# Nine of twelve wide weight slabs multiplied unsplit in fp32, eight slots for the modulation units, and x loaded later

## Chip, core and metric

The kernel runs on one core of one Trainium2 chip. The metric is the device time of one launch in microseconds. Before the change three runs took 1018.0, 1018.48 and 1018.72 us; their median is 1018.48 us. PE is TensorE, DVE is VectorE, ACT is ScalarE, POOL is GpSimd, and SP is SyncE, whose only work here is to issue loads.

## What is computed

A decoder trunk of two layers over 256 tokens of 2048 features. Each layer has a modulation vector from `c`, a normalised and modulated input `h`, one wide input projection, two branches, a gate and an output projection:

```python
c_act = jax.nn.silu(c)
for l in range(DEPTH):
    mod = c_act @ ada_w[l] + ada_b[l]
    shift, scl, gate_res = jnp.split(mod[:, None, :], 3, axis=-1)
    h = _rms(x, norm_g[l]) * (1.0 + scl) + shift
    ...
        z = h @ ev_w_in[e]
        ...
    x = x + gate_res * ((y * jax.nn.silu(g)) @ w_out[l])
```

All inputs are fp32. What matters here is the beginning: `h` of the first layer needs the first third of the modulation (`scl` and `shift`, 4096 columns of a 2048-row matrix), and the first projection `z = h @ ev_w_in` needs `h`.

## The kernel before

Everything lies transposed: features on the 128 partitions, the 256 tokens along the free axis. `X` holds x in 16 chunks of 128 features.

**Weights.** The projections are cut into 141 slabs of 1 MB (2048 rows by 128 columns). A slab is loaded in two halves of 512 KB (eight 128x128 blocks each) into `raw`, which has four half slots. ACT rounds each half to fp32r, `whi` (`hi`, L400), DVE computes the rest, `wlo = raw - whi` (`lo`, L1027). `h` is split in the same way into `hhi` (ACT, L418) and `hlo` (DVE, L1112). PE multiplies each block three times in fp32r: whi by hhi, whi by hlo, wlo by hhi (L724, L726, L727 in the wide stage).

**Modulation.** The matrix comes in pieces of 1024 columns, each in 16 units of 512 KB; the first four pieces (units 0 to 63) are the shifts and scales of the first layer. DVE multiplies each unit by its value of `c_act` and adds it to `acc` (`add_units`, L1038, and for piece 3 in two halves of 512 columns, `half_units`, L1055 and L1058). When 16 units are in, PE sums over the partitions (`reduce_part`, L761), and DVE adds the bias (`keep_piece`, L1062), makes the gain, scales x (`norm_x`, L1105) and finishes `h` (`make_h`). Each piece gives four chunks of `h`. Units have four slots of `ada`; SP may load unit n when unit n-4 has been added.

**The wide stage.** The first 12 slabs are multiplied together, `h` chunk by chunk (`wide_chunk`): a chunk is 12 blocks, its 12 sums stay in six PSUM banks. So PE can begin with chunks 0 to 3 (group 0, 48 blocks, six halves of `raw`) when piece 0 is known, goes on with chunks 4 to 7 (group 1) after piece 1 and with chunks 8 to 11 (group 2) after piece 2. Chunks 12 and 13 need the first half of piece 3, chunks 14 and 15 the second. Blocks lie in the slabs in the order in which the stage uses them, so "slab w" of this stage is just the w-th megabyte. A group is three slabs.

**The order of the work.** Every engine follows an order written out by hand, with semaphores. SP's queue is one line: a load whose wait is not met holds back all the loads behind it. In DVE's order, the first four units of the next piece stand ahead of the group of `h` (`add_units(UNITS * p, 4, None)`, then `group_of_h(p - 1)`). PE sends the count `pe_half` at the end of each half of `raw` that it has used; it starts at 4. After a group's last block PE runs `keep_warm`, multiplications of constants that keep it occupied, and then waits for the piece. After the wide stage each of the other 129 slabs is multiplied in turn.

## Time and profile before

| | before |
|---|---|
| median of three runs | 1018.48 us |
| the profiled execution | 1017.85 us, of it a span of 1016.1 us |
| PE busy | 955.8 us, 94% |
| DVE busy | 835.2 us, 82% |
| ACT busy | 437.3 us, 43% |
| POOL busy | 46.7 us, 5% |
| moved by DMA | 261.32 MB, mean 257 GB/s |
| mean granted clock of PE | 0.985 |

Time runs from the span's start. "Idle before" is the time for which an engine stood before an instruction, and the arrow names what ended it. Matmuls are pipelined: the duration of one is longer than the distance to the next, so prices of PE are read from starts. An fp32 multiplication (not fp32r) leaves two records, an fp32r one leaves one: the 16 statistics steps of two fp32 multiplications each have 64 records at L740.

### The profile page before, as it was taken

The page shows a single profiled execution, that of the slowest core. Times are in us where ns is not written, and L with a number is a line of the kernel's source. Part 1 is how long each engine was busy: PE and PEld are TensorE (multiplying, and loading weights), DVE is VectorE, ACT ScalarE, POOL GpSimd, SP SyncE. Part 2 cuts the span into 40 slices and gives each one's busy share as a digit, 9 for nine tenths or more (in the row PEclk, how much of TensorE's full clock was granted, in tenths as well). Part 3 has the DMA queues.
Part 4 walks back from the last instruction along what each step waited for, and adds up shares of the span by engine and source line. Part 5 has one row for each costly group of instructions (what it writes and reads, how often), then busy time and mean ns, then how long its engine had stood idle before and what let it go on. Part 6 is the DMA issues. An engine that isn't in the chain of part 4 may idle for free.

```text
span 1016.1 us, 20238 instructions
## 1 busy us (share of the span) xinstructions
PE 955.8 (94%) x7728; PEld 945.8 (93%) x7728; DVE 835.2 (82%) x1244; ACT 437.3 (43%) x693; POOL 46.7 (5%) x63
## 2 busy tenths in 40 slices
PE   5197799999999999999999999999999999999997
PEld 5197789999999999999999999999999999999997
DVE  4898987987899778887877898888999986878842
ACT  4122125434555444333344444444446555743331
POOL 1000000011010000000000000000010100000000
PEclk9997798999999999999999999999999999999999
DMA  8999988989777888899857755544445555588961
GB/s 337 339 325 360 324 296 316 321 287 369 290 275 243 279 285 287 312 359 362 312 189 269 242 196 180 189 137 162 150 162 180 167 172 199 196 309 307 342 220 41
DMA packets 71094, 261.32 MB, mean 257 GB/s; under 512 B 7904, under 2 KB 8032, under 8 KB 70768
## 3 DMA queue, kind: packets, MB, share of 16 engines
q1 hardware_dynamic: 68544, 250.86, 70.0%
q0 software_dynamic: 2480, 9.50, 2.6%
q8 instruction: 47, 0.77, 0.3%
q14 instruction: 23, 0.19, 0.1%
HBM read 256.07 MB, written 4.19 MB: 256 GB/s over the span
## 4 chain that ended last, share of the span: by engine, by line
PE 77%; DVE 14%; DMA 4%; issue 3%; ACT 2%; SPq 0%; DVEq 0%; POOL 0%; ACTq 0%; POOLq 0%
PE bank L707 20%; PE bank L708 19%; PE bank L709 19%; DVE acc L1038 6%; DVE wlo L1027 3%; PE bank L809 3%; DMA ada<-ada_units 3%; PE bank L812 3%; PE bank L811 3%; PE bank L724 1%; PE bank L726 1%; PE bank L727 1%; PE bank L777 1%; DVE X L1105 1%; ACT whi L400 1%
## 5 line engine op out<-in xcount | busy, mean ns | idle before, releaser
L400 ACT ACTIVATE whi<-raw 128x1024 fp32r<-128x1024 f32 x282 | 297.2, 1060 | 447.6 <-PE bank L709 338.5
L1027 DVE TENSOR_TENSOR wlo<-raw,whi 128x1024 fp32r<-128x1024 f32 x282 | 341.4, 1224 | 91.9 <-ACT whi L400 91.3
L707 PE MATMUL bank<-hhi,whi 128*128 128x256 f32 x1168 | 337.1, 289 | 2.3 <-ACT T L619 0.9
L708 PE MATMUL bank<-hlo,whi 128*128 128x256 f32 x1168 | 330.4, 283 | 0.0
L709 PE MATMUL bank<-hhi,wlo 128*128 128x256 f32 x1168 | 330.3, 283 | 0.0
L1038 DVE SCALAR_TENSOR_TENSOR acc<-ada,cact,acc 128x1024 f32<-128x1024 f32 x176 | 226.1, 1285 | 33.0 <-DMA ada<-ada_units 16.5
L707 PEld LDWEIGHTS bank<-hhi,whi 128*128 128x128 f32 x1168 | 223.9, 192 | 5.7 <-issue 3.8
L708 PEld LDWEIGHTS bank<-hlo,whi 128*128 128x128 f32 x1168 | 224.1, 192 | 0.1
L709 PEld LDWEIGHTS bank<-hhi,wlo 128*128 128x128 f32 x1168 | 223.8, 192 | 0.0
L707 PE MATMUL bank<-ghi,whi 128*128 128x256 f32 x512 | 147.9, 289 | 0.0
L708 PE MATMUL bank<-glo,whi 128*128 128x256 f32 x512 | 144.9, 283 | 0.0
L709 PE MATMUL bank<-ghi,wlo 128*128 128x256 f32 x512 | 144.8, 283 | 0.0
L724 PE MATMUL bank<-hhi,whi 128*128 128x256 f32 x320 | 95.9, 300 | 20.5 <-DVE hlo L1112 20.5
L1238 DVE SCALAR_TENSOR_TENSOR Y<-U,par,Y 128x256 f32<-128x256 f32 x240 | 98.6, 480 | 0.0
L707 PEld LDWEIGHTS bank<-ghi,whi 128*128 128x128 f32 x512 | 98.3, 192 | 0.0
L708 PEld LDWEIGHTS bank<-glo,whi 128*128 128x128 f32 x512 | 98.3, 192 | 0.0
L709 PEld LDWEIGHTS bank<-ghi,wlo 128*128 128x128 f32 x512 | 98.2, 192 | 0.0
L726 PE MATMUL bank<-hlo,whi 128*128 128x256 f32 x320 | 94.7, 296 | 0.0
L727 PE MATMUL bank<-hhi,wlo 128*128 128x256 f32 x320 | 94.4, 295 | 0.0
L724 PEld LDWEIGHTS bank<-hhi,whi 128*128 128x128 f32 x320 | 65.8, 206 | 21.1 <-DVE hlo L1112 21.1
L809 PE MATMUL bank<-whi,hhi 128*128 128x256 f32 x256 | 73.8, 288 | 0.0
L812 PE MATMUL bank<-wlo,hhi 128*128 128x256 f32 x256 | 72.4, 283 | 0.0
(166 smaller groups left out, 1070.1 us busy)
## 6 DMA issues: line engine op xcount, KB each, us to landing
raw<-w_slabs SPq DMA_DIRECT2D x282, 512.0 KB, 4.9
ada<-ada_units SPq DMA_DIRECT2D x192, 512.0 KB, 6.3
X<-xT SPq DMA_DIRECT2D x1, 2048.0 KB, 7.6
x_dram<-X POOLq DMA_DIRECT2D x4, 512.0 KB, 5.4
outT<-X POOLq DMA_DIRECT2D x4, 512.0 KB, 5.0
V<-pool_w POOLq DMA_DIRECT2D x1, 1024.0 KB, 6.2
U<-xT POOLq DMA_DIRECT2D x2, 512.0 KB, 9.8
V<-xT POOLq DMA_DIRECT2D x2, 512.0 KB, 7.4
```

Of the source, the lines that this page charges most:

```text
L400: act.activation(whi[:, slot], raw[:, slot], ACT.Copy).then_inc(hi_done, 1)
L707: mm(out, whi[:, s, k, :], ahi[:, c, :], start=(c == 0), stop=False)
L708: mm(out, whi[:, s, k, :], alo[:, c, :], start=False, stop=False)
L709: last = mm(out, wlo[:, s, k, :], ahi[:, c, :], start=False, stop=(c == KC - 1))
L724: mm(wide(s), whi[:, slot, k, :], hhi[:, c, :], start=(c == 0 and s % 2 == 0), stop=False, skip_group_check=True)
L726: mm(wide(s), whi[:, slot, k, :], hlo[:, c, :], start=False, stop=False, skip_group_check=True)
L727: last = mm(wide(s), wlo[:, slot, k, :], hhi[:, c, :], start=False, stop=(c == KC - 1), skip_group_check=True)
L809: mm(out, hhi[:, c, tokens], upper, start=(c == 0 and q == 0), stop=False, skip_group_check=True)
L812: last = mm(out, hhi[:, c, tokens], lower, start=False, stop=(c == KC - 1), skip_group_check=True)
L1027: dve.tensor_tensor(wlo[:, s], raw[:, s], whi[:, s].bitcast(F32), ALU.subtract)\
L1038: dve.scalar_tensor_tensor(acc[:, p % 2, :], ada[:, slot, :], cact[:, bass.ds(k, 1)], acc[:, p % 2, :], ALU.mult, ALU.add).then_inc(ada_do ...
L1238: ins = dve.scalar_tensor_tensor(Y[:, j, :], U[:, j, k:k + SEQ], par[:, wcol:wcol + 1], Y[:, j, :], ALU.mult, ALU.add)
```

## The change

It has four parts.

1. Chunks 0 to 11 (144 blocks, slabs 0 to 8) are multiplied once, in fp32, straight from `raw` and from `X`, in which ACT completes `h` in place (`unsplit_chunk`, `full_h`). Their `hi` and `lo` are gone. `hhi` and `hlo` of these chunks are still made, for the later slabs. Chunks 12 to 15 (slabs 9 to 11) stay split.
2. Units 0 to 63 go round eight slots: four of `ada`, two of `V`, two of `Y`. Unit n may be loaded when unit n-8 has been added.
3. `x` is loaded behind units 0 to 3 rather than ahead of all units.
4. SP's order and its waits are new: slabs 2 to 10 wait for `pe_half`, which means that PE has used the half four places earlier. In each of the pieces 1 to 3 the queue holds 8 units, a slab, 3 units, a slab, 4 units, a slab, 1 unit.

```diff
@@ -39,6 +39,7 @@
 GROUP = 4
+FIRST = 4 * UNITS
 
...
@@ -49,6 +50,9 @@
 WIDE = (12, 8)
+
+
+UNSPLIT = 9
 
...
@@ -216,6 +221,24 @@
 
+        def unit_slot(n):
+
+            return n % 8 if n < FIRST else n % 4
+
+        def unit_uses(n, t):
+
+            uses = n // 8 + 1 if n < FIRST else FIRST // 8 + (n - FIRST) // 4 + 1
+            return uses if t is None else uses + t
+
+        def unit_at(n):
+
+            slot = unit_slot(n)
+            if slot < 4:
+                return ada[:, slot, :]
+            if slot < 6:
+                return V[:, slot - 4, :]
+            return Y[:, 4 * (slot - 6):4 * (slot - 5), :].rearrange("p a t -> p (a t)")
+
         def half_slot(w, half):
...
@@ -242,31 +265,44 @@
         def _(sp):
-            sp.sem_inc(lo_done, 4)
+            sp.sem_inc(lo_done, 4 + 2 * UNSPLIT)
             sp.sem_inc(ada_done, 4)
             sp.dma_start(par[:], params).then_inc(par_in, 16)
-            sp.dma_start(X[:], xT).then_inc(x_in, 16)
-
             def load_units(n, count, t):
                 for u in range(count):
-                    slot = (n + u) % 4
                     unit = n + u if t is None else n + u + 4 * t
-                    sp.wait_ge(ada_done, unit + 1)
-                    sp.dma_start(ada[:, slot, :], ada_units[bass.ds(unit, 1)].rearrange("a p n -> p (a n)"))\
-                      .then_inc(ada_in[slot], 16)
+                    if n >= FIRST:
+                        sp.wait_ge(ada_done, unit + 1)
+                    elif unit >= 8:
+                        sp.wait_ge(ada_done, unit - 3)
+                    sp.dma_start(unit_at(n + u), ada_units[bass.ds(unit, 1)].rearrange("a p n -> p (a n)"))\
+                      .then_inc(ada_in[unit_slot(n + u)], 16)
 
             def load_slab(w, t):
                 for half in range(2):
                     slot = half_slot(w, half)
-                    sp.wait_ge(lo_done, 2 * now(w, t) + half + 1)
+                    if w >= UNSPLIT + 2:
+                        sp.wait_ge(lo_done, 2 * now(w, t) + half + 1)
+                    elif w >= 2:
+                        sp.wait_ge(pe_half, 2 * w + half + 1)
                     sp.dma_start(raw[:, slot], w_slabs[bass.ds(now(w, t), 1), :, 8 * half:8 * half + 8, :]
                                  .rearrange("a p k n -> p (a k) n")).then_inc(raw_in[slot], 16)
 
-            for p in range(4):
-                for part in range(4):
-                    load_units(UNITS * p + 4 * part, 4, None)
-                    if part < 3 and 3 * p - 1 + part >= 0:
-                        load_slab(3 * p - 1 + part, None)
+            load_units(0, 4, None)
+            sp.dma_start(X[:], xT).then_inc(x_in, 16)
+            load_units(4, 4, None)
+            load_slab(0, None)
+            load_units(8, 4, None)
+            load_slab(1, None)
+            load_units(12, 4, None)
+            for p in range(1, 4):
+                load_units(UNITS * p, 8, None)
+                load_slab(3 * p - 1, None)
+                load_units(UNITS * p + 8, 3, None)
+                load_slab(3 * p, None)
+                load_units(UNITS * p + 11, 4, None)
+                load_slab(3 * p + 1, None)
+                load_units(UNITS * p + 15, 1, None)
             load_slab(WIDE[0] - 1, None)
...
@@ -385,6 +421,7 @@
             act.sem_inc(pe_half, 4)
+            act.sem_inc(hi_done, 2 * UNSPLIT)
             n = [0]
...
@@ -396,7 +433,8 @@
                     act.wait_ge(raw_in[slot], 16 * half_uses(w, half, t))
-                    act.wait_ge(pe_half, 2 * now(w, t) + half + 1)
+                    if w >= UNSPLIT + 2:
+                        act.wait_ge(pe_half, 2 * now(w, t) + half + 1)
                     act.activation(whi[:, slot], raw[:, slot], ACT.Copy).then_inc(hi_done, 1)
...
@@ -410,6 +448,15 @@
                 act.activation(T[:, i % 2, :], X[:, j, :], ACT.Square).then_inc(sq_done, 1)
+
+            def full_h(chunks):
+                for j in chunks:
+                    col = shift_col(0, j)
+                    act.wait_ge(xr_done, j + 1)
+                    act.activation(X[:, j, :], X[:, j, :], ACT.Identity, bias=mod[:, col:col + 1])\
+                       .then_inc(h_done, 1)
+                    act.wait_ge(h_done, j + 1)
+                    act.activation(hhi[:, j, :], X[:, j, :], ACT.Copy).then_inc(hhi_done, 1)
 
...
@@ -506,24 +553,19 @@
                 square_x(j, j)
-            hi(0, None)
-            hi(1, None)
             root(0, QT)
             act.wait_ge(spread, 1)
             act.activation(DS[:, 0, 0:SEQ], XB[:, 0:SEQ], ACT.Copy).then_inc(r_copied, 1)
 
-            for g in range(3):
-                upper_h(0, range(GROUP * g, GROUP * (g + 1)))
-                hi(3 * g + 2, None)
-                hi(3 * g + 3, None)
-                if g < 2:
-                    hi(3 * g + 4, None)
+            full_h(range(0, 12))
+            hi(9, None)
             upper_h(0, range(12, 14))
             hi(10, None)
             upper_h(0, range(14, 16))
             hi(11, None)
             hi(12, None)
             act.wait_ge(pe_half, 2 * WIDE[0] + 4)
+            act.wait_ge(hlo_done, KC)
             for s in range(8):
...
@@ -725,6 +767,19 @@
                     last = mm(wide(s), wlo[:, slot, k, :], hhi[:, c, :], start=False, stop=(c == KC - 1),
+                              skip_group_check=True)
+                    if k == 7:
+                        last.then_inc(pe_half, 1)
+
+            def unsplit_chunk(c):
+
+                pe.wait_ge(h_done, c + 1)
+                for s in range(WIDE[0]):
+                    half, k = (WIDE[0] * c + s) // 8, (WIDE[0] * c + s) % 8
+                    slot = half_slot(0, half)
+                    if s == 0 or k == 0:
+                        pe.wait_ge(raw_in[slot], 16 * half_uses(0, half, None))
+                    last = mm(wide(s), raw[:, slot, k, :], X[:, c, :], start=(c == 0 and s % 2 == 0), stop=False,
                               skip_group_check=True)
...
@@ -888,7 +943,7 @@
                         ins.then_inc(half_sum, 1)
-                    wide_chunk(0, U0, c)
+                    unsplit_chunk(c)
             wide_chunk(0, U0, 12)
...
@@ -1030,12 +1085,11 @@
                     unit = first + u if t is None else first + u + 4 * t
-                    slot, p = (first + u) % 4, first // UNITS
-                    uses = (first + u) // 4 + 1
+                    p = first // UNITS
                     k = unit - UNITS * p
-                    dve.wait_ge(ada_in[slot], 16 * (uses if t is None else uses + t))
+                    dve.wait_ge(ada_in[unit_slot(first + u)], 16 * unit_uses(first + u, t))
                     dve.wait_ge(ada_done, unit + 4)
-                    dve.scalar_tensor_tensor(acc[:, p % 2, :], ada[:, slot, :], cact[:, bass.ds(k, 1)],
+                    dve.scalar_tensor_tensor(acc[:, p % 2, :], unit_at(first + u), cact[:, bass.ds(k, 1)],
                                              acc[:, p % 2, :], ALU.mult, ALU.add).then_inc(ada_done, 1)
...
@@ -1109,6 +1163,10 @@
                 dve.wait_ge(hhi_done, KC * layer + j + 1)
+                if layer == 0 and j < 12:
+                    dve.tensor_tensor(hlo[:, j, :], X[:, j, :], hhi[:, j, :].bitcast(F32), ALU.subtract)\
+                       .then_inc(hlo_done, 1)
+                    return
                 dve.scalar_tensor_tensor(hlo[:, j, :], X[:, j, :], mod[:, col:col + 1],
...
@@ -1269,13 +1327,8 @@
                 add_units(UNITS * p + 4, 4, None)
-                if p:
-                    lo(3 * p - 1, None)
                 add_units(UNITS * p + 8, 4, None)
-                lo(3 * p, None)
-                add_units(UNITS * p + 12, 2, None)
-                lo(3 * p + 1, None)
-                add_units(UNITS * p + 14, 2, None)
+                add_units(UNITS * p + 12, 4, None)
                 if p == 0:
...
@@ -1285,7 +1338,6 @@
             half_units(52, 4)
-            lo(8, None)
             half_units(56, 4)
```

The same move as the program's order shows it. SP's queue of the kernel before, from the load of x to the last units of piece 1 and the first of piece 2 (the last row); `ada<-ada_units` is a unit, `raw<-w_slabs` a half slab, `X<-xT` the load of x:

```order
L248 DMA X<-xT 128x4096
L255 DMA ada<-ada_units 128x1024 x8
L262 DMA raw<-w_slabs 128x1024 x2
L255 DMA ada<-ada_units 128x1024 x4
L262 DMA raw<-w_slabs 128x1024 x2
L255 DMA ada<-ada_units 128x1024 x8
L262 DMA raw<-w_slabs 128x1024 x2
L255 DMA ada<-ada_units 128x1024 x4
L262 DMA raw<-w_slabs 128x1024 x2
L255 DMA ada<-ada_units 128x1024 x4
L262 DMA raw<-w_slabs 128x1024 x2
L255 DMA ada<-ada_units 128x1024 x8
```

And the same queue after the change, up to unit 15 (units in `V` and `Y` are loaded under those names):

```order
L270 DMA par<-params 128x428
L278 DMA ada<-ada_units 128x1024 x4
L292 DMA X<-xT 128x4096
L278 DMA V<-ada_units 128x1024 x2
L278 DMA Y<-ada_units 128x1024 x2
L288 DMA raw<-w_slabs 128x1024 x2
L278 DMA ada<-ada_units 128x1024 x4
L288 DMA raw<-w_slabs 128x1024 x2
L278 DMA V<-ada_units 128x1024 x2
L278 DMA Y<-ada_units 128x1024 x2
```

x has moved behind four units; both slabs 0 and 1 stand ahead of the last four units of piece 0, as before.

SP's queue after the change from unit 27 to the first units of piece 2, the end of a group's loads; the second `raw` row here is slab 4, whose halves wait until PE has used the fifth and the sixth half of group 0, the latter being the group's last:

```order
L288 DMA raw<-w_slabs 128x1024 x2
L278 DMA ada<-ada_units 128x1024
L278 DMA V<-ada_units 128x1024 x2
L278 DMA Y<-ada_units 128x1024
L288 DMA raw<-w_slabs 128x1024 x2
L278 DMA Y<-ada_units 128x1024
L278 DMA ada<-ada_units 128x1024 x4
L278 DMA V<-ada_units 128x1024 x2
```

Unit 31, the last of piece 1 (the single `Y`), and units 32 to 35, the four `ada` behind it, stand behind slab 4. Before, units 28 to 35 stood behind slab 4 too, but there slab 4 waited for DVE's `lo` of slab 2, not for PE's last half.

DVE's order from the group of `h` after piece 0 to the one after piece 1, before:

```order
L1112 SCALAR_TENSOR_TENSOR hlo<-X,mod,hhi 128x256 x3
L1038 SCALAR_TENSOR_TENSOR acc<-ada,cact,acc 128x1024 x4
L1027 TENSOR_TENSOR wlo<-raw,whi 128x1024 x2
L1038 SCALAR_TENSOR_TENSOR acc<-ada,cact,acc 128x1024 x4
L1027 TENSOR_TENSOR wlo<-raw,whi 128x1024 x2
L1038 SCALAR_TENSOR_TENSOR acc<-ada,cact,acc 128x1024 x2
L1027 TENSOR_TENSOR wlo<-raw,whi 128x1024 x2
L1038 SCALAR_TENSOR_TENSOR acc<-ada,cact,acc 128x1024 x6
L1062 TENSOR_TENSOR mod<-bank,par 128x8
```

And after:

```order
L1167 TENSOR_TENSOR hlo<-X,hhi 128x256 x3
L1092 SCALAR_TENSOR_TENSOR acc<-V,cact,acc 128x1024 x2
L1092 SCALAR_TENSOR_TENSOR acc<-Y,cact,acc 128x1024 x2
L1092 SCALAR_TENSOR_TENSOR acc<-ada,cact,acc 128x1024 x4
L1092 SCALAR_TENSOR_TENSOR acc<-V,cact,acc 128x1024 x2
L1092 SCALAR_TENSOR_TENSOR acc<-Y,cact,acc 128x1024 x2
L1092 SCALAR_TENSOR_TENSOR acc<-ada,cact,acc 128x1024 x4
L1116 TENSOR_TENSOR mod<-bank,par 128x8
```

The six `lo` are gone; the sixteen adds, the last four of them units of the next piece, have stayed ahead of the group of `h`.

## Rows read from the trace of the kernel before

**Rows 1.** The page: busy PE and its granted clock in 40 slices, and DVE's `lo`

```profile
PE   5197799999999999999999999999999999999997
...
PEclk9997798999999999999999999999999999999999
...
L1027 DVE TENSOR_TENSOR wlo<-raw,whi 128x1024 fp32r<-128x1024 f32 x282 | 341.4, 1224 | 91.9 <-ACT whi L400 91.3
```

**Rows 2.** Waits from 0 to 165 us: total us, times, longest

```profile
PE bank L724 <- DVE hlo L1112: 20.5, 5, 6.6
```

**Rows 3.** Waits of PE from 165 us to the end, the longest one

```profile
PE bank L844 <- DVE SP L1222: 1.9, 4, 0.8
```

**Rows 4.** Timeline of PE: start us, us, instruction, idle before and its releaser

```profile
51.10 0.58 PE L724 MATMUL bank<-hhi,whi 128*128 128x256 f32 x1 [4.75 <-DVE hlo L1112]
...
51.91 0.41 PE L724 MATMUL bank<-hhi,whi 128*128 128x256 f32 x1
...
52.12 0.41 PE L726 MATMUL bank<-hlo,whi 128*128 128x256 f32 x1
...
56.33 0.28 PE L724 MATMUL bank<-hhi,whi 128*128 128x256 f32 x1
...
70.72 0.94 PE L694 MATMUL bank<-ident,ones 128*128 128x128 f32 x7
...
85.25 0.58 PE L724 MATMUL bank<-hhi,whi 128*128 128x256 f32 x1 [6.40 <-DVE hlo L1112]
...
104.87 1.39 PE L694 MATMUL bank<-ident,ones 128*128 128x128 f32 x11
...
119.63 0.58 PE L724 MATMUL bank<-hhi,whi 128*128 128x256 f32 x1 [6.63 <-DVE hlo L1112]
...
139.89 0.28 PE L727 MATMUL bank<-hhi,wlo 128*128 128x256 f32 x1
...
140.81 0.39 PE L724 MATMUL bank<-hhi,whi 128*128 128x256 f32 x1 [0.64 <-DVE hlo L1112]
...
149.67 1.05 PE L761 MATMUL bank<-ones,acc 128*128 128x1 f32 x8
...
152.82 0.58 PE L724 MATMUL bank<-hhi,whi 128*128 128x256 f32 x1 [2.10 <-DVE hlo L1112]
...
163.97 0.28 PE L727 MATMUL bank<-hhi,wlo 128*128 128x256 f32 x1
```

**Rows 5.** Timeline of PE, fp32 multiplications of 128x256, two records each

```profile
821.62 3.62 PE L999 MATMUL bank<-Y,ones 128*128 128x256 f32 x16
...
185.02 1.97 PE L789 MATMUL bank<-Y,V 128*128 128x256 f32 x8
```

**Rows 6.** Stretches of 2 us: busy time by engine, granted clock, DMA share, GB/s

```profile
26.00:28.00 2.00, 0.00 (x0) 0.00 (x0) 1.79 (x3) 0.00 (x0) 0.00 (x0) 1.00 1.03 422
48.00:50.00 2.00, 0.00 (x0) 0.00 (x0) 1.93 (x5) 0.10 (x1) 0.00 (x0) 1.00 1.01 336
```

**Rows 7.** A load issued into an idle queue at 11 us: size, us to landing

```profile
ada<-ada_units SPq DMA_DIRECT2D x1, 512.0 KB, 3.6
```

**Rows 8.** Timeline of SP, its first load

```profile
0.88 0.39 SPq L247 DMA_DIRECT2D par<-params  x1
```

**Rows 9.** Timeline of DVE, as Rows 4

```profile
38.97 1.28 DVE L1038 SCALAR_TENSOR_TENSOR acc<-ada,cact,acc 128x1024 f32<-128x1024 f32 x1
...
43.60 5.46 DVE L1038 SCALAR_TENSOR_TENSOR acc<-ada,cact,acc 128x1024 f32<-128x1024 f32 x4 [1.73 <-ACT DS L513]
...
50.57 0.48 DVE L1112 SCALAR_TENSOR_TENSOR hlo<-X,mod,hhi 128x256 fp32r<-128x256 f32 x1
...
111.13 0.75 DVE L1055 SCALAR_TENSOR_TENSOR acc<-ada,cact,acc 128x512 f32<-128x512 f32 x1
...
112.77 0.75 DVE L1055 SCALAR_TENSOR_TENSOR acc<-ada,cact,acc 128x512 f32<-128x512 f32 x1
...
148.86 0.75 DVE L1058 SCALAR_TENSOR_TENSOR acc<-ada,cact,acc 128x512 f32<-128x512 f32 x1
```

More of the change, by code:

```diff
@@ L156, in build @@
         raw_in = [sem(f"raw_in{i}") for i in range(4)]
-        ada_in = [sem(f"ada_in{i}") for i in range(4)]
+        ada_in = [sem(f"ada_in{i}") for i in range(8)]
         hi_done = sem("hi_done")
@@ L182, in build @@
         xr_done = sem("xr_done")
+        h_done = sem("h_done")
         hhi_done = sem("hhi_done")
@@ L1049, in half_units @@
                 for unit in range(first, first + count):
-                    slot, u, p = unit % 4, unit % UNITS, unit // UNITS
+                    u, p, half = unit % UNITS, unit // UNITS, PIECE // 2
                     out = acc[:, p % 2, PIECE // 2 * (u // 8):PIECE // 2 * (u // 8 + 1)]
                     k = 2 * (u % 8)
-                    dve.wait_ge(ada_in[slot], 16 * (unit // 4 + 1))
+                    dve.wait_ge(ada_in[unit_slot(unit)], 16 * unit_uses(unit, None))
                     dve.wait_ge(ada_done, unit + 4)
-                    seq(dve.scalar_tensor_tensor(out, ada[:, slot, 0:PIECE // 2], cact[:, k:k + 1], out,
+                    seq(dve.scalar_tensor_tensor(out, unit_at(unit)[:, 0:half], cact[:, k:k + 1], out,
                                                  ALU.mult, ALU.add))
                     settle()
-                    dve.scalar_tensor_tensor(out, ada[:, slot, PIECE // 2:], cact[:, k + 1:k + 2], out,
+                    dve.scalar_tensor_tensor(out, unit_at(unit)[:, half:], cact[:, k + 1:k + 2], out,
                                              ALU.mult, ALU.add).then_inc(ada_done, 1)
```

## The prediction

> **What bounds the kernel now.** I first looked at the 40 slices of the page [rows 1]: PE's idle time lies in the first slices, in the first 165 us, and it is busy in nearly all that follow; its clock dips in the same place. The waits say what it lacks there: 20.5 us in five waits for `hlo` [rows 2]. From 165 us on its longest wait sums to 1.9 us [rows 3]. So from there on PE is the bound, and what moves the end of the wide stage moves the end of the kernel by as much. I therefore work out one number: when the wide stage ends, against 164.1 us now.
>
> The timeline of PE gives the stage now [rows 4]. Group 0 starts at 51.10 and its last multiplication is out at 70.72 (19.6 us). Group 1 runs from 85.25 to 104.87 (19.6). Group 2 runs from 119.63 to 140.0 (20.4, with four reductions in it). Chunks 12 and 13 start at 140.81, chunks 14 and 15 at 152.82. Between the groups lie 14.5 us and 14.8 us. A group begins on the slow clock: two multiplications are 0.21 us apart at 51.91, and from 56.33 the other 40 blocks take 14.4 us, 0.36 us a block. The slow part is 5.2 us. These two paces are the two levels, 1.2 and 2.4 GHz, and the clock fell while PE waited.
>
> **Start of group 0.** Before unit 15 can be added, the queue has to move x (four times 512 KB), 16 units and four half slabs: 24 transfers of 512 KB, and 0.2 MB of parameters. With all DMA engines occupied it moved 422 GB/s in one stretch and 336 in another [rows 6], 1.24 to 1.56 us for a transfer. I take 1.3, nearer to the fast row, since that one is from the stretch that this term is about. With eight slots the queue doesn't run dry here. A load into an idle queue lands after 3.6 us [rows 7], so about 2.3 of it are not transfer; I split them into 1.2 ahead of the first byte and 1.1 behind the last. The first load is issued at 0.88 [rows 8], the first byte moves at 2.1. Then 2.1 + 0.6 + 24 x 1.3 + 1.1 + 1.3 (the add) gives 36.3 us for the end of unit 15. Now it is 38.97 + 1.28 = 40.25 [rows 9]. That is 3.9 us earlier (1.24 would give 5.3, 1.56 nothing or a loss of 2). x itself lands by 14 us, and its 16 statistics are hidden by the units. What follows (root, spread, four adds of 5.46 us, the gain) is as before, but PE then waits for ACT's `h` and not for `hlo`, whose 0.5 us [rows 9] drops out. **Term 1: -4.4 us**; group 0 starts at 46.7.
>
> **The groups of PE.** An fp32 multiplication of 128x256 leaves two records. Sixteen records take 3.62 us, and less the last one's 0.38 that is 15 distances of 0.216: 0.432 us for a block. The other row gives 7 distances in 1.59, 0.454 a block [rows 5]. Split, a block costs 0.36. So unsplit is dearer for PE, by 0.07 us at full clock. I take 0.432 (the longer row, less blurred by its ends). On the slow clock I estimate twice that, 0.86. In the 5.2 slow us PE then does 6 blocks, and 42 more take 18.1: 23.3 us for a group instead of 19.6. Three groups: **term 2: +11.1 us** (at 0.454, +13.9).
>
> The Trainium skill, FP8 and Floating Point Precision, TensorE Precision Notes, says that true fp32 makes four passes through the array; TensorE: Matmul & The Clock Gate, Back-to-back issue gap, gives a pass of N columns N/2.4 ns + 2.5. By the two pages that is 437 ns a block against 328 for three passes, so an estimate of 109 ns more for each of 144 blocks, 15.7 us; the rows say 0.07 us at full clock, since the split multiplications run slower here than that formula has it. For the fp32 block row and formula agree within 0.005 us. The sum goes by the rows.
>
> **From the end of a group to the next.** What leaves: DVE's 18 `lo` at 1.22 us [rows 1], 22 us over the stage, of which up to three stand in each gap. This would be the gain, if DVE still set the pace. But SP's waits change. Call T the end of a group's PE work. Slab 4's second half waits for the sixth half used, so SP issues it at T, unit 31 at T + 0.5, units 32 to 35 behind. Slab 4's first half was issued at T - 3.5, units 27 to 30 at T - 6.4 to - 5.0, slab 3's second half at T - 6.9, all paced by eight blocks of 0.432. From T - 5.7 on the queue therefore works without a pause through eight transfers (slab 3's half, four units, two halves, unit 31): T + 4.7, and unit 31 lands at T + 5.8. Units 32 to 35 follow; DVE adds one in 1.39 us (5.46 for four [rows 9]), and the fifth add ends at T + 12.7. Bias, gain, scaling and `h` take 1.5 (now 2.0 from the end of the four adds at 49.06 to 51.10, less the `hlo`): group 1 starts at T + 14.2, where it is T + 14.5 now. For group 2 the four adds ahead are of the half kind, 1.64 us each (111.13 to 112.77 [rows 9]), so T + 15.2, against 14.8. **Term 3: -0.3 + 0.4 = +0.1 us.** Lower bound: into an idle queue unit 31 lands at T + 4.1, and the gaps are 12.6 and 13.6, together 3.1 us under those of now.
>
> DVE, with its `lo` gone, now idles in the middle of the groups: its 16 adds of 1.39 us are 22 us in a cycle of 37. It waits for units that stand in the queue behind slabs, and those wait for PE.
>
> **Chunks 12 to 15.** Units 59 to 62 stand behind slab 9, whose second half waits until PE has used 32 blocks of group 2 (T - 7.9 with the reductions). Unit 59 lands at about T - 3 and is added by T - 1.4. Then come the two `lo` of slab 9 (2.3 us), bias, gain, the first chunk's `h` and `hlo` (2.1, as the 2.0 ahead of group 0): chunk 12 starts at T + 3.0. Now it starts 0.8 us behind group 2, since DVE is ahead. **Term 4: +2.2 us.** From there DVE runs through two units, the `lo` of slab 10, two units and the last of `h`: the same work as now, 12.2 us to chunk 14 instead of 12.0. **Term 5: +0.2 us.** Chunks 14 and 15 are unchanged.
>
> **Sum.** -4.4 + 11.1 + 0.1 + 2.2 + 0.2 = +9.2 us. The profiled execution took 1017.85 us (a span of 1016.1 and 1.75 around it), so it would take 1027.05; it is 0.63 under the median of the runs. On the median's footing: 1018.48 + 9.2 = **1027.7 us**. In the stage, group 1 should start near 84, group 2 near 123, chunk 12 near 150, chunk 14 near 162, and the end lie near 173.3.
>
> Hidden or nothing: ACT's 18 `hi` go, but no row shows PE held by ACT here. ACT now does two steps for each chunk of `h` instead of one; at an estimated 0.4 to 0.5 us for the second (as DVE's step of the same shape [rows 9]) DVE's group of `h` lasts some 1.6 us longer, and DVE's idle time covers it. It would cost 1.6 us a group only if DVE had none. Adds from `V` and `Y` have the same shape as those from `ada`. `V` is next written by the load of pool weights, behind piece 3.
>
> **Rivals.**
> A. *A dearer stage*: chunk 12 starts cold as well. PE waits 3.0 us ahead of it. In the gap of 3.1 us ahead of chunk 14 the clock now falls: the start at 152.82 is as slow as that at 51.10 (0.58 us for the first in both) [rows 4]. Chunks 12 and 13 would take 11.2 rather than 8.7 us and end at T + 14.2, later than DVE's last unit; chunk 14 comes 2 us later: 1029.7. Likewise a queue at 1.4 us a transfer: 2.4 us on term 1, 0.8 on each gap, 1031.7; for it speaks the row of 336 GB/s. Chance 0.24.
> B. *The adds run ahead* (the other side). If SP could issue units 31 to 35 before the group's end, as eight slots would let it, DVE would have added them all by T. A gap would be keep-warm (48 records at 0.11 us by the row at 70.72, 5.3 us), the reduction (16 records, 2 us by the row at 149.67) and 1.5 for `h`: 9 us. That is 5.2 and 6.2 less than in my sum, and term 4 goes too: -4.4 us, 1014. It decides if slab 4's second half is issued 4 us or more before T. Against it: its wait is for the group's last half, and the order puts it ahead. The same side would be reached if an fp32 block cost under 0.432 - 9.2/144 = 0.37 us; both rows of fp32 are above that. Chance 0.10.
> C. *Little change*: the queue at 1.24 us or better throughout, and gaps at their lower bound. Term 1 becomes -5.8, term 3 -3.1: +4.6 us, 1023, and with term 4 at nothing 1021. For it: the row of 422 GB/s and the idle queue of [rows 7]. Chance 0.11, half of it below 1020.5.
> D. *The clock stays low through whole groups* of fp32: 48 x 0.86 = 41 us, 18 more for each, 1081. At 821 us the fp32 rows stand in a slice of full clock [rows 1, 5], so they don't pull it down; that they raise it no row shows. Chance 0.03.
>
> **How the numbers follow.** My forecast (1024.5 to 1029.5) has 0.52. The range 1020.5 to 1032 takes in the forecast, nearly all of A and half of C, 0.8. A measurement here can't tell 0.2%, 2 us, from no change. Slower: 0.52 + 0.24 + 0.03 + half of C = 0.84; same: the other half of C, 0.06; faster: B, 0.10.
>
> **What would show it.** Right: two records of 0.216 us for each wide block; the `raw` loads at eight-block steps through a group and a queue idle between; DVE waiting for `ada`, `V` or `Y` loads in the groups; unit 31 landing about 5 us after a group's last block; starts at the times above. Wrong: a group under 22 us, a gap under 12, a start of group 0 later than 49, or PE waits after 175 us that are shorter than now, which would mean that the loss is given back.

## The result: 1032.88 us, 1.6% slower, and the profile after

The changed kernel takes 1032.88 us in the median of 4 runs (1031.4 to 1035.07), the kernel before 1018.24 beside it (4 runs): a ratio of 1.0156, 95% interval 1.0136 to 1.0177. Forecast were 1027.7 us and a range up to 1032.0, so the direction was right and the size too small, by 5.2 us. The profiled execution took 1035.07 us (span 1033.3), the slowest of the four. Its profile is compared with one of 1017.85 us, so it shows 17.2 us of difference where the medians show 14.6.

PE's slices on the page, with the granted clock and the share of the DMA engines, for [rows 1]:

```profile
PE   4497688999999999999999999999999999999997
...
PEclk9998898999999999999999999999999999999999
DMA  9776877888787687899966665544445355588961
...
L782 PE MATMUL bank<-X,raw 128*128 128x256 f32 x288 | 69.5, 406 | 13.4 <-ACT X L456 13.4
```

The hole in the first slices has remained and reaches two slices further: before, the slices under 9 end with the fifth, now with the seventh. The new line is the fp32 multiplication, 288 records for 144 blocks, and PE waits for ACT's `X` (the completed `h`) in place of `hlo`. The waits of PE from 180 us to the end, the longest, for [rows 3]:

```profile
PE bank L899 <- DVE SP L1280: 1.9, 4, 0.8
```

It is the wait of before. Behind the wide stage nothing is given back: from the stage's end the kernel runs 851 to 852 us in both traces. So 16.6 of the 17.2 us lie in the stage. The timeline of PE there, with columns as in [rows 4]:

```profile
47.03 23.62 PE L782 MATMUL bank<-X,raw 128*128 128x256 f32 x96 [4.10 <-ACT X L456]
...
71.81 5.62 PE L736 MATMUL bank<-ident,ones 128*128 128x128 f32 x48 [1.16 <-DVE acc L1092]
79.45 3.37 PE L816 MATMUL bank<-ones,acc 128*128 128x1 f32 x16 [2.02 <-DVE acc L1092]
86.37 22.73 PE L782 MATMUL bank<-X,raw 128*128 128x256 f32 x96 [3.55 <-ACT X L456]
...
127.02 17.71 PE L782 MATMUL bank<-X,raw 128*128 128x256 f32 x72 [5.79 <-ACT X L456]
...
145.38 5.43 PE L782 MATMUL bank<-X,raw 128*128 128x256 f32 x24
156.42 0.58 PE L766 MATMUL bank<-hhi,whi 128*128 128x256 f32 x1 [5.62 <-DVE hlo L1170]
...
170.48 0.38 PE L766 MATMUL bank<-hhi,whi 128*128 128x256 f32 x1 [2.10 <-DVE hlo L1170]
...
181.65 0.39 PE L749 MATMUL bank<-hhi,whi 128*128 128x256 f32 x1 [0.80 <-ACT U L570]
```

The groups end at 70.65, 109.10 and 150.81. The last row is the start of the next stage, 165.06 us before: 16.6 us later. The gaps are 15.7 and 17.9 us (14.5 and 14.8 before). What stands in a gap is seen in SP's timeline and, below it, in DVE's:

```profile
60.32 3.78 SPq L288 DMA_DIRECT2D raw<-w_slabs  x2
64.15 0.43 SPq L278 DMA_DIRECT2D ada<-ada_units  x1
64.62 0.90 SPq L278 DMA_DIRECT2D V<-ada_units  x2
65.57 0.96 SPq L278 DMA_DIRECT2D Y<-ada_units  x1
67.23 3.78 SPq L288 DMA_DIRECT2D raw<-w_slabs  x2
71.05 0.43 SPq L278 DMA_DIRECT2D Y<-ada_units  x1
```

```profile
61.99 1.28 DVE L1092 SCALAR_TENSOR_TENSOR acc<-ada,cact,acc 128x1024 f32<-128x1024 f32 x1 [6.14 <-DMA ada<-ada_units]
70.47 1.28 DVE L1092 SCALAR_TENSOR_TENSOR acc<-ada,cact,acc 128x1024 f32<-128x1024 f32 x1 [4.37 <-DMA ada<-ada_units]
...
78.11 1.28 DVE L1092 SCALAR_TENSOR_TENSOR acc<-Y,cact,acc 128x1024 f32<-128x1024 f32 x1 [2.19 <-DMA Y<-ada_units]
...
117.74 1.28 DVE L1092 SCALAR_TENSOR_TENSOR acc<-Y,cact,acc 128x1024 f32<-128x1024 f32 x1 [3.28 <-DMA Y<-ada_units]
...
150.63 0.75 DVE L1109 SCALAR_TENSOR_TENSOR acc<-ada,cact,acc 128x512 f32<-128x512 f32 x1 [4.27 <-DMA ada<-ada_units]
```

Slab 4's two halves are issued 3.45 us apart (the pair lasts 3.78 us, its last issue 0.33 of that), eight blocks of 0.431 us: SP's queue goes at PE's pace. Unit 31 is issued right behind, 0.4 us after the group's end, and lands at 78.11, 7.5 us after that end; unit 47 lands 8.6 us after its group's, and unit 59 with the end of group 2. DVE, freed of its `lo`, waits for all three. In the waits of SP up to 180 us the first row is new:

```profile
SPq L288 <- PE bank L782: 76.9, 18, 16.2
SPq L278 <- DVE acc L1092: 32.4, 25, 4.2
```

SP's queue stands 77 us for slabs that wait for PE, most of it with units behind them; before, PE held it nowhere.

When a load lands is its issue in SP's timeline plus its time to landing. For slab 3's two halves (issued at 60.32 and 63.77) and for unit 27 (issued at 64.15) that time is:

```profile
raw<-w_slabs SPq DMA_DIRECT2D x1, 512.0 KB, 5.6
...
raw<-w_slabs SPq DMA_DIRECT2D x1, 512.0 KB, 5.4
...
ada<-ada_units SPq DMA_DIRECT2D x1, 512.0 KB, 6.3
```

They land at 65.9, 69.2 and 70.5. From unit 27 to unit 31 (DVE's rows at 70.47 and 78.11) six loads land in 7.64 us, 1.27 us each; from the landing of `x` (14.8) to that of unit 22 (44.2) the 23 loads came 1.28 us apart. Ahead of slab 3's second half, though, nothing landed for 3.2 us, 2.0 us more than a load takes at that pace. I call this a pause. The stretches, columns as in [rows 6], show it as three slow microseconds (65 to 68) between two stretches of full pace:

```profile
15.00:44.00 29.00, 18.21 (x84) 18.07 (x84) 20.21 (x22) 8.21 (x19) 0.94 (x1) 1.00 1.03 408
62.00:65.00 3.00, 3.00 (x16) 2.64 (x15) 2.74 (x3) 0.00 (x0) 0.00 (x0) 1.00 1.02 414
65.00:68.00 3.00, 3.00 (x16) 2.64 (x15) 1.10 (x1) 0.00 (x0) 0.00 (x0) 1.00 0.84 262
69.00:77.00 8.00, 6.84 (x54) 6.31 (x53) 5.14 (x4) 0.00 (x0) 0.00 (x0) 1.00 1.03 416
```

The loads ahead of unit 47 had two pauses: slab 6's second half lands 3.0 us behind the load ahead of it, slab 7's second half 2.3 us. What makes a pause no run here shows.

### The profile page after: what moved, and what is told of

Read it like the earlier page. It is cut to its first block, busy times and chain, and to the rows that moved or that the text cites. A ratio compares the mean times of both kernels' runs of the same rounds, so it can differ in the third digit from the quotient of the medians.

```text
span 1033.3 us, 19905 instructions
## 1 busy us (share of the span) xinstructions
PE 969.0 (94%) x7584; PEld 949.1 (92%) x7584; DVE 815.3 (79%) x1226; ACT 423.0 (41%) x687; POOL 46.7 (5%) x63
## 4 chain that ended last, share of the span: by engine, by line
PE 80%; DVE 10%; DMA 6%; issue 2%; ACT 2%; SPq 0%; DVEq 0%; POOL 0%; ACTq 0%; POOLq 0%
PE bank L749 19%; PE bank L750 18%; PE bank L751 18%; PE bank L782 5%; DMA ada<-ada_units 3%; DVE acc L1092 3%; PE bank L864 3%; PE bank L866 3%; PE bank L867 3%; DVE wlo L1082 3%; DMA V<-ada_units 3%; PE bank L832 1%; PE bank L795 1%; PE bank L816 1%; DVE X L1159 1%
## 5 line engine op out<-in xcount | busy, mean ns | idle before, releaser
L438 ACT ACTIVATE whi<-raw 128x1024 fp32r<-128x1024 f32 x264 | 278.1, 1060 | 422.0 <-PE bank L751 339.8
L1082 DVE TENSOR_TENSOR wlo<-raw,whi 128x1024 fp32r<-128x1024 f32 x264 | 319.9, 1224 | 88.9 <-ACT whi L438 88.3
L749 PE MATMUL bank<-hhi,whi 128*128 128x256 f32 x1168 | 337.1, 289 | 3.0 <-DVE wlo L1082 1.2
L750 PE MATMUL bank<-hlo,whi 128*128 128x256 f32 x1168 | 330.4, 283 | 0.0
L751 PE MATMUL bank<-hhi,wlo 128*128 128x256 f32 x1168 | 330.3, 283 | 0.0
L1092 DVE SCALAR_TENSOR_TENSOR acc<-ada,cact,acc 128x1024 f32<-128x1024 f32 x152 | 195.3, 1285 | 43.9 <-DMA ada<-ada_units 30.7
L749 PEld LDWEIGHTS bank<-hhi,whi 128*128 128x128 f32 x1168 | 223.9, 192 | 6.3 <-issue 3.8
L782 PE MATMUL bank<-X,raw 128*128 128x256 f32 x288 | 69.5, 406 | 13.4 <-ACT X L456 13.4
L782 PEld LDWEIGHTS bank<-X,raw 128*128 128x128 f32 x288 | 58.9, 206 | 22.7 <-ACT X L456 13.7
L866 PE MATMUL bank<-whi,hlo 128*128 128x256 f32 x256 | 72.4, 283 | 0.0
L766 PE MATMUL bank<-hhi,whi 128*128 128x256 f32 x176 | 51.9, 295 | 7.7 <-DVE hlo L1170 7.7
```

The source lines that it names most:

```text
L438: act.activation(whi[:, slot], raw[:, slot], ACT.Copy).then_inc(hi_done, 1)
L749: mm(out, whi[:, s, k, :], ahi[:, c, :], start=(c == 0), stop=False)
L750: mm(out, whi[:, s, k, :], alo[:, c, :], start=False, stop=False)
L751: last = mm(out, wlo[:, s, k, :], ahi[:, c, :], start=False, stop=(c == KC - 1))
L766: mm(wide(s), whi[:, slot, k, :], hhi[:, c, :], start=(c == 0 and s % 2 == 0), stop=False, skip_group_check=True)
L782: last = mm(wide(s), raw[:, slot, k, :], X[:, c, :], start=(c == 0 and s % 2 == 0), stop=False, skip_group_check=True)
```

## The experiments

Each is timed beside the kernel before. Its median was 1018.28 us beside the first four, 1017.56 beside the last two and the kernel with 8 keep-warm multiplications, and 1018.22 beside the others. T is the end of a group's multiplications.

**The units ahead of slab 4.** SP's order alone is changed:

```diff
-            for p in range(1, 4):
-                load_units(UNITS * p, 8, None)
...
-            load_slab(WIDE[0] - 1, None)
+            for first, count, w in ((16, 12, 2), (28, 4, 3), (32, 4, 4), (36, 8, 5), (44, 4, 6), (48, 4, 7),
+                                    (52, 8, 8), (60, 4, 9), (64, 0, 10), (64, 0, WIDE[0] - 1)):
+                load_units(first, count, None)
+                load_slab(w, None)
```

> The changed kernel with another order of SP's loads alone: units 16 to 27 ahead of slab 2, 28 to 31 ahead of slab 3, 32 to 35 ahead of slab 4 and so on, so that no unit of a piece stands behind a slab that waits for the end of a group. Theory 1 (units held back behind slabs that wait for PE): the gaps from a group's end to the next fall from 15.9 and 18.1 us to about 9 (keep-warm, reduction, h), chunk 12 follows group 2 within 1 to 2 us; the kernel takes 1013 to 1017 us. Theory 2 (the bytes and the dearer fp32 blocks set the pace, the queue would be as full anyway): gaps stay above 13 us, 1028 us or more.

Measured: 1012.59 us (5 runs), ratio 0.9952 (0.9937 to 0.9967), 20.3 us less than with the order of the change. PE's timeline:

```profile
46.77 23.31 PE L777 MATMUL bank<-X,raw 128*128 128x256 f32 x96 [4.11 <-ACT X L451]
69.92 5.52 PE L731 MATMUL bank<-ident,ones 128*128 128x128 f32 x48
75.28 1.84 PE L811 MATMUL bank<-ones,acc 128*128 128x1 f32 x16
78.64 22.67 PE L777 MATMUL bank<-X,raw 128*128 128x256 f32 x96 [1.52 <-ACT X L451]
...
109.87 17.31 PE L777 MATMUL bank<-X,raw 128*128 128x256 f32 x72 [1.52 <-ACT X L451]
...
135.61 0.39 PE L761 MATMUL bank<-hhi,whi 128*128 128x256 f32 x1 [2.35 <-DVE hlo L1165]
...
158.58 0.39 PE L744 MATMUL bank<-hhi,whi 128*128 128x256 f32 x1 [0.80 <-ACT U L565]
```

The groups are as long as in the changed kernel. The gaps are 8.6 us, made of keep-warm, reduction and 1.5 us for `h`, with no wait for a load in them. SP still waits 57.7 us for PE, but what stands behind the slabs is no longer urgent. This is rival B's mechanism at its price (9 us), and it shows the cause: not that slabs wait for PE, but that the next group's units queue behind them.

**Unit 31 alone ahead of slab 4.**

```diff
-                load_slab(3 * p + 1, None)
                 load_units(UNITS * p + 15, 1, None)
+                load_slab(3 * p + 1, None)
```

> The changed kernel with the last unit of each of the pieces 1 to 3 issued ahead of the slab that waits for the group's end, and nothing else. Units 32 to 35 (48 to 51) still stand behind that slab, and DVE adds them before it makes h. Theory 1a (all five units behind the slab count, the last of them ends the gap): within 2 us of the changed kernel, 1031 to 1034. Theory 1b (the piece's last unit and PE's reduction end the gap): 2 to 3 us less in each of two gaps, 1027 to 1029.

Measured: 1033.85 us, 1.0155 (1.013 to 1.0179). Groups 1 and 2 start at 86.86 and 126.08. DVE still has to add units 32 to 35 ahead of `h`, and they are still held: moving one unit buys nothing.

**Four slots in the changed kernel.** `FIRST = 0`.

> The changed kernel with the modulation units in four slots of ada as before (unit n waits for unit n-4), everything else as changed. If eight slots carry part of the result: group 0 starts 2 to 3 us later and each gap grows by 1 to 2 us, since units 33 to 35 wait for adds: 1035 to 1039. If the waits of the slabs hold the queue anyway and slots count for nothing: 1032 to 1034.

Measured: 1031.96 us, 1.0141 (1.0121 to 1.0162); starts at 46.93, 85.39, 126.09. With this order the eight slots are worth nothing, and not at the start of group 0 either.

**Slots and late x in the split kernel.** Parts 2 and 3 of the change in the kernel before, with its order and its split.

> The kernel before with eight slots and with x loaded behind units 0 to 3, the 12 slabs split as before, SP's order and slab waits as before. If the slots and the late x are a gain by themselves, group 0 starts 2 to 3 us earlier than at 51.1 and the DMA waits of 0.9 us in each gap go: 1014 to 1016.5. Rival: DVE's order of adds and lo sets the starts, 1017.5 to 1019.

Measured: 1015.09 us (7 runs), 0.9966 (0.9951 to 0.9981). Group 0 starts at 49.79 instead of 51.10.

**x loaded first, in the changed kernel.**

```diff
+            sp.dma_start(X[:], xT).then_inc(x_in, 16)
...
-            load_units(0, 4, None)
-            sp.dma_start(X[:], xT).then_inc(x_in, 16)
-            load_units(4, 4, None)
+            load_units(0, 8, None)
```

> The changed kernel with x loaded ahead of all units, as before; nothing else. Unit 0 comes 5 us later, but unit 15 stands behind the same 24 transfers of 512 KB. If the queue sets the start of group 0 (my term 1), nothing changes: within 2 us of the changed kernel (1031 to 1035), group 0 starts at 47 again. If the late x is a gain by itself: group 0 starts 2 us or more later.

Measured: 1033.22 us, 1.0155 (1.0131 to 1.0179); group 0 starts at 46.52. The bytes ahead of unit 15 are the same, and here their order doesn't matter.

**Keep-warm ahead of chunk 12.** `keep_warm(24, M)` between chunks 11 and 12 of the changed kernel, for rival A.

> The changed kernel with 24 keep-warm multiplications of PE between group 2 and chunk 12, in the gap of 5.8 us, and nothing else. If the slow clock at chunk 12's start is what makes chunk 14 come 14.1 us behind it instead of 12.2 (rival A of the prediction): chunk 14 follows chunk 12 by about 12 us, and the kernel is 1.5 to 2.5 us faster than the changed one, 1030 to 1031.5. If DVE's chain sets chunk 14: no change.

Measured: 1031.49 us, 1.0138 (1.0113 to 1.0163). The 1.4 us less in the median is within the intervals. The place itself is clear: chunk 12 starts at 158.23 with 0.36 us for its first record, where the changed kernel has 0.58, and chunk 14 follows 11.8 us later, not 14.1. DVE's row that takes the sums of the piece in between:

```profile
167.94 0.16 DVE L1117 TENSOR_TENSOR mod<-bank,par 128x4 f32<-128x4 f32 x1 [1.69 <-PE bank L816]
```

It waits 1.69 us for PE's sums, against 3.19 in the changed kernel: there the chunks 12 and 13, begun at 1.2 GHz, held DVE, as rival A says. From chunk 12 to the next stage the trace has 21.5 us instead of 25.2; the median shows less of it, and in this trace chunk 12 itself starts 1.8 us later.

**Units ahead, and no keep-warm in the gaps.** The order of the first experiment, `keep_warm(24, M)` ahead of the reductions taken out.

> The kernel with the units ahead of the slabs (e_units_ahead), without the 24 keep-warm multiplications ahead of the reduction of pieces 1 and 2. There the gaps of 8.7 us consist of keep-warm (5.4), reduction (1.8) and h (1.5). If keep-warm stands on the path: gaps of 3.4 us, less what DVE's adds of units 32 to 35 need (they end 6.8 us behind the group's end in the first gap, so about 8 us there and 3.4 in the second), 1007 to 1010 us. If DVE's adds set both gaps or a colder clock eats it: 1011 to 1013.

Measured: 1010.75 us, 0.9932 (0.9908 to 0.9956), the fastest median of all. The gaps fall by 0.5 and 0.9 us only (PE's second group and the row ahead of it):

```profile
70.06 1.84 PE L811 MATMUL bank<-ones,acc 128*128 128x1 f32 x16
78.28 22.80 PE L777 MATMUL bank<-X,raw 128*128 128x256 f32 x96 [6.38 <-ACT X L451]
```

The wait for `h` is 6.4 us instead of 1.5: keep-warm had covered DVE's four adds and `h`. With 8 instead of 24:

> The order with the units ahead and 8 instead of 24 keep-warm multiplications ahead of each reduction: between the 1012.6 us of 24 and the 1010.8 us of none. If the gap is set by DVE's adds once keep-warm is shorter than about 4 us, the time is that of none, 1010 to 1012, and the next group starts on the fast clock for a shorter slow part; 1009.5 at best.

Measured: 1011.64 us, 0.9933 (0.9908 to 0.9958). Between 0, 8 and 24 the medians lie in order, but the three intervals overlap: no number of them is shown to be better.

**The split kernel with the units ahead.** Its slots and late x, with the order of the first experiment.

> The kernel before (12 slabs split), with eight slots, x behind units 0 to 3 and the order of loads of e_units_ahead. If unsplit multiplication pays once the loads are free (it takes 22 us of lo from DVE and adds 10 us to PE): this one stays slower than e_units_ahead, near e_slots_split, 1014 to 1016 us. If the order of the loads is all of the gain: 1010 to 1013, the same as e_units_ahead.

Measured: 1022.96 us (8 runs), 1.0051 (1.0033 to 1.0068). The waits up to 165 us:

```profile
ACT whi L420 <- DMA raw<-w_slabs: 35.9, 11, 6.7
...
PE bank L744 <- DVE hlo L1131: 16.9, 5, 5.0
```

Now slabs come late for `hi` and `lo`, which stand ahead of adds on DVE. The same order costs the split kernel 7.9 us (1015.09 to 1022.96) and gives the unsplit one 20.3: order and split belong together.

**Half the bytes ahead of unit 31.** For units 27 to 30, 43 to 46 and 59 to 62:

```diff
+                    if n < FIRST and n >= UNITS and n % UNITS == 11:
+                        sp.dma_start(unit_at(n + u)[:, 0:512],
+                                     ada_units[bass.ds(unit, 1), :, 0:512].rearrange("a p n -> p (a n)"))\
+                          .then_inc(ada_in[unit_slot(n + u)], 16)
+                        continue
```

> The changed kernel, but the loads of units 27 to 30, 43 to 46 and 59 to 62 bring only the first 512 of 1024 columns (256 KB for 512 KB); the adds keep their size, so the second half of their slots is older data and the modulation is not the reference's. If unit 31 lands late because the bytes ahead of it move at 1.3 to 1.6 us for 512 KB, four half transfers less take 2.6 to 3.2 us off its landing (T+7.6 becomes T+4.4 to T+5, T+8.8 becomes T+5.6 to T+6.2), the gaps of 15.9 and 18.1 us become about 13 and 15, chunk 12 starts 2 us earlier, and the kernel takes 1024 to 1027 us. The rival: after the queue has been idle, the delay goes by the number of transfers or is a fixed cost of starting again; then unit 31 lands less than 1 us earlier and the time stays at 1031 to 1033.

The second half of each of these units is then older data, so this kernel doesn't compute the reference's modulation. Measured: 1029.43 us, 1.0112 (1.0082 to 1.0142), 3.5 us less, between the two theories. Unit 31 lands at T + 6.2 (7.5 without the edit), unit 47 at T + 6.0 (8.6): 1.3 and 2.6 us earlier, where bytes alone would give 2.6 to 3.2. In the first gap it is then unit 32 that DVE waits for, 1.56 us, and the gap stays 15.9 us; the second is 15.3. The landings, one by one, tell why in the first gap it is only 1.3 (issue plus time to landing, in us; in brackets the distance to the load ahead, worked out before rounding):

| load | changed kernel | half bytes |
|---|---|---|
| slab 3, first half | 65.9 | 66.0 |
| slab 3, second half | 69.2 (3.2) | 69.6 (3.6) |
| unit 27 | 70.5 (1.3) | 70.3 (0.7) |
| unit 28 | 71.7 (1.3) | 71.0 (0.7) |
| unit 29 | 73.0 (1.3) | 71.7 (0.7) |
| unit 30 | 74.3 (1.3) | 72.3 (0.6) |
| slab 4, first half | 75.5 (1.3) | 73.6 (1.3) |
| slab 4, second half | 76.8 (1.3) | 75.7 (2.1) |
| unit 31 | 78.1 (1.3) | 77.0 (1.3) |

Two of the rows behind it, both of this kernel: the time to landing of unit 27 (issued at 64.27) and of slab 4's second half (issued at 70.81):

```profile
ada<-ada_units SPq DMA_DIRECT2D x1, 256.0 KB, 6.0
...
raw<-w_slabs SPq DMA_DIRECT2D x1, 512.0 KB, 4.9
```

A half load takes half the time, 0.6 to 0.7 us where a whole one takes 1.3, and the four together save 2.4 us. The rest is pauses: the one ahead of slab 3's second half is 0.4 us longer, and there is a new one of 0.8 us ahead of slab 4's.

**The four units ahead of slab 3.** `load_units(UNITS * p + 8, 7, None)` and then both slabs and unit 31.

> The changed kernel with units 27 to 30 (43 to 46, 59 to 62) put ahead of slab 3 (6, 9), so that only that slab, slab 4 and one unit stand behind PE's halves. The bytes to be moved from T-13.8 on to unit 31 are the same, so if the queue's pace alone counts, unit 31 lands at most 0.5 us earlier and the time stays at 1031 to 1033 us; slab 3 may come late instead. If what counts is how many transfers are handed over in the last 7 us ahead of T (six then two), unit 31 lands about T+4 to T+5, the gaps fall by 3 us each and the kernel takes 1025 to 1028.

Measured: 1032.66 us, 1.0141 (1.0117 to 1.0165). Unit 31 lands at T + 7.2, unit 47 at T + 7.5. Units 27 to 30 land early, but slab 4's second half lands at 73.5 and unit 31 at 76.5, 3.0 us behind it. Here the pause stands ahead of unit 31 itself, though the DMA engines move at full pace throughout:

```profile
59.00:69.00 10.00, 10.00 (x48) 8.81 (x47) 7.70 (x6) 0.00 (x0) 0.00 (x0) 1.00 1.02 413
69.00:77.00 8.00, 5.67 (x50) 5.45 (x48) 1.80 (x2) 0.00 (x0) 0.00 (x0) 1.00 1.03 408
```

Without its pause of 1.7 us unit 31 would land at T + 5.5, as in the changed kernel without its 2.0 (T + 7.5 less 2.0). So how many loads are handed over last seems not to matter, and the full pace of the engines doesn't tell when one load lands.

## Why the prediction came out too low

**Term 1** (-4.4 us): measured -4.1. DVE's last add of unit 15 ends at 36.8 us, predicted 36.3. The queue was the bound, as forecast, at 1.28 us a load. But it would have been without late x (46.5) and with four slots (46.9) as well, and in the split kernel both together bring 1.3 us. The rest is read from the traces alone: 0.6 us is the `hlo` for which PE no longer waits, and 2.1 us, the largest part, are the `lo` of DVE. Before, four of them stood between the adds of units 11 and 15, and now none:

```profile
30.41 2.36 DVE L1027 TENSOR_TENSOR wlo<-raw,whi 128x1024 fp32r<-128x1024 f32 x2
...
35.32 2.35 DVE L1027 TENSOR_TENSOR wlo<-raw,whi 128x1024 fp32r<-128x1024 f32 x2
```

**Term 2** (+11.1): measured 23.62 + 22.73 + 23.79 against 59.6 for the three, +10.5. The block costs 0.431 us as [rows 5] said. Rival D fell: the stream of fp32 raises the clock as the split one did, after 5.3, 3.6 and 3.9 us at 1.2 GHz in the three groups (by the starts of their records), where the sum had 5.2 for each. The estimate of 0.437 us a block from the Trainium skill (FP8 and Floating Point Precision, TensorE Precision Notes, with TensorE: Matmul & The Clock Gate, Back-to-back issue gap) agrees with the trace; the step from three passes to four that the same formula gives, 0.109 us, does not: the trace shows 0.07.

**Term 3** (+0.1): measured +1.2 and +3.1, +4.3 in all. This is the step that failed, in the words of the prediction: "the queue therefore works without a pause through eight transfers ...: T + 4.7, and unit 31 lands at T + 5.8". The eight transfers were the right ones, and their pace, 1.27 us, was close to the 1.3 counted; "without a pause" is what was wrong. Between slab 3's first half and unit 31 the landings span 12.1 us, of which 2.0 are the pause ahead of slab 3's second half; ahead of unit 47 they span 13.0, with pauses of 1.7 and 1.0. So the units landed at T + 7.5 and T + 8.6 instead of T + 5.8, 1.7 + 2.8 = 4.5 us. What follows the landing was right: 8.3 and 9.3 us to the group's start, predicted 8.4 and 9.4.

The 1.3 was taken for term 1, from the faster of [rows 6]. The trace of before could have told that loads come unevenly inside a group: its group 0 (48 to 64 us), beside the stretch from which the 1.3 came (20 to 36), columns as in [rows 6]:

```profile
48.00:64.00 16.00, 12.90 (x89) 12.90 (x89) 14.09 (x19) 5.00 (x7) 0.00 (x0) 1.00 1.01 363
20.00:36.00 16.00, 3.30 (x16) 3.21 (x16) 12.72 (x11) 6.69 (x8) 0.00 (x0) 1.00 1.02 404
```

At the same share of busy DMA engines, 363 GB/s is 1.44 us a transfer on average and 404 is 1.30. In the first stretch the loads issued at 46.32 and 47.71 landed at 51.2 and 53.3, 2.1 us apart. With 1.44 us, unit 31 would have been put at T + 6.9, with the 1.56 of the slow row of [rows 6] at T + 7.9.

[rows 7] was also misread, and with it the lower bound of term 3: the queue wasn't idle. The load ahead was issued at 3.4 and took 10.6 us, so it landed at 14.0, while the one of the row was issued at 11.7. A load into a queue that is empty took 3.1 us (slab 2's first half, issued at 53.41 in the changed kernel).

**Term 4** (+2.2): measured 5.6 us behind group 2 against 0.8, +4.8. The same mistake once more: "Unit 59 lands at about T - 3" was T - 0.2. Slab 9's two halves, the loads ahead of it, landed 3.2 us apart (146.1 and 149.2). The `lo`, gain and `h` behind it are as worked out: 5.8 us from the landing to chunk 12.

**Term 5** (+0.2): measured 14.06 us against 12.0, +2.05. Here rival A was right: PE had waited 5.6 us, chunk 12 started at 1.2 GHz (0.58 us), and chunk 14 came 1.9 us later than forecast. Chunks 14 and 15 took 1.1 us less than before, since they had only 3.4 us at 1.2 GHz (from 171.9 us) and not 5.7.

Together -4.1 + 10.5 + 4.3 + 4.8 + 2.05 - 1.1 = 16.5 us, the shift of the next stage (16.6). Forecast were 9.2. The 7.3 missing are 4.2 of term 3, 2.6 of term 4 and 1.9 of rival A, less 1.3 elsewhere. So the step that failed is the queue without a pause, in terms 3 and 4; rival A came on top, with PE waiting 5.6 us ahead of chunk 12 where the sum had 3.0. Rival A's other half, a queue at 1.4 us a transfer, didn't come true: it would have cost 2.4 us on term 1, which lost 0.3.

The mechanism stands: the freed DVE time was turned into a wait for loads in SP's queue, and one change of order takes out 20 us. Open is what makes the pauses.

## What to carry to other kernels

When a split or any other work is taken off an engine, look at what its loads wait for in its place: a slab that waits for PE at the head of a shared queue stops every load behind it, and what is put behind should be what is needed last. More slots help only where the queue's order lets them be filled: the eight slots gave nothing with one order, and the other order gave 20 us. Whether that order needs eight of them no run shows. When a burst of loads behind a wait is costed, its pace is not enough: look at the landings one by one for pauses, leave room for one or two of them, and add up the rivals that share a cause.

## What the runs showed of the hardware

First, loads of 512 KB in one queue landed 1.27 to 1.28 us apart, at 408 to 416 GB/s, with single pauses of 0.8 to 2.8 us in between (0.8 in the table above; 2.8 in the run with unit 31 ahead, where slab 3's second half landed at 69.6, 4.0 us behind the first). In the changed kernel none came among the 23 loads from 14.8 to 44.2 us, and one or more in each of the three bursts that followed an empty queue. A running group of fp32 doesn't slow the queue by itself. In the kernel with the units ahead, the rest of group 1 and the gap behind it, a stretch inside group 0, and the slow microseconds behind that:

```profile
92.00:114.00 22.00, 20.48 (x120) 18.59 (x119) 16.53 (x24) 3.37 (x8) 0.95 (x1) 0.92 1.03 412
60.00:65.00 5.00, 5.00 (x25) 4.41 (x24) 4.47 (x4) 0.00 (x0) 0.00 (x0) 1.00 1.01 410
65.00:68.00 3.00, 3.00 (x16) 2.64 (x15) 1.82 (x2) 0.00 (x0) 0.00 (x0) 1.00 0.86 294
```

The cause of the pauses is left open. Second, PE's fp32 stream brings the granted clock from 1.2 to 2.4 GHz as a split stream does: in group 1 with the units ahead, begun at 78.64, it reads 0.50 in the first row and 1.00 in the second:

```profile
80.00:82.00 2.00, 2.00 (x6) 1.62 (x5) 1.15 (x3) 1.52 (x4) 0.00 (x0) 0.50 1.03 412
84.00:86.00 2.00, 2.00 (x11) 1.77 (x10) 1.90 (x2) 0.00 (x0) 0.00 (x0) 1.00 0.98 365
```
